# Branch A's scores as two runs of 320 keys in two banks, its filler stages by halves in one bank

## The chip, the cores and the metric

The kernel runs on one core of a Trainium2 chip. The metric is the device time of one launch in microseconds (us), median of the runs. TensorE (PE, with its weight loads shown as PEld) multiplies, VectorE (DVE), ScalarE (ACT) and GpSimd (POOL) work beside it, SyncE (SP) issues weight transfers. Each engine works through its own queue in order, and engines meet by semaphores only.

## The reference

One step of a two-layer backbone (DEPTH 2, width 1024) on 128 context tokens and 512 latent tokens, 640 in all, which is five tiles of 128 (tile 0 context, tiles 1 to 4 latent). Every layer has one input projection that feeds three branches. Branch A, which the change is about, is:

```
def dense_gqa(q, k, v, n_kv, sink=None):          # 8 query heads, 2 key/value heads, head_dim 64
    s = einsum('bqkgd,blkd->bkgql', qblk, k)      # 128 queries at a time
    p = softmax(s)
    return einsum('bkgql,blkd->bqkgd', p, v)
# latent:  a_out = dense_gqa(qa, concat([ka, ka_ctx]), concat([va, va_ctx]), 2)   512 + 128 cached keys
# context: a_out = dense_gqa(qa, ka, va, 2)                                       128 keys
# merge:   g_a, g_b, g_c = split(sigmoid(h @ w_gate + b_gate)); y = (g_a*ya + g_b*yb + g_c*yc) @ w_out
```

Branch B is windowed attention with cached keys and a sink, branch C a gated mixing of chunks. Matrix products are done to nearly full float32 precision by splitting operands into a rounded high part and a low remainder, both fp32r, and multiplying high by high, high by low and low by high.

## The kernel before

All engines walk one written order, `ORDER`, of events such as `("S", l, br, g, i)`; every engine does its own part of each event, in that order. So the place of an event in the order is its place in every queue. A plan (`bank_plan`) gives each stage that TensorE fills one or two of the 8 PSUM banks; TensorE waits (`begin`) until the stage that held the bank before has been read (`wait_drained`).

Branch A works on ten groups of four heads: `GROUPS` are (key/value head, query tile) pairs, tiles 1, 2, 3, 4 for groups 0 to 7 and tile 0 for groups 8 and 9. A latent group has 5 key tiles (4 latent, 1 cached), a context group 1. `attention` makes one step for each key tile of each group, 42 steps in all. Before step 0 stands the entry, with the first scores. Step n holds, in this order:

- `T`: four transposes of the probabilities (PE), which ACT then copies rounded to `p_hi`; DVE makes the remainder (`pl`)
- `S`: at most one score unit of a later group in most steps (PE); DVE takes the maxima and writes `neg`
- `iv`: the inverse of the sum of the unit scored one step before (DVE), and POOL's product of the probabilities with it
- the `O`, `og`, `oh`, `ol` events that finish an output, where due
- `PV`: the two products with the values of step n-2 (PE, `L1110` and `L1111`)
- the filler: work of another stage that keeps TensorE busy
- `ex`: the exponentials of the unit scored in this step (ACT)

The filler of branch A is the gate product of the merge, `z`: seven stages `("z", l, 0, j)`, j from 1 to 7, each 48 matmuls of 320 columns (both halves of the 640 tokens) in 8 chunks of 6 matmuls. A stage takes two banks (6 and 7) and ACT copies both halves out with one instruction (L1365) at the `z` event behind the last chunk. 8 chunks lie in the entry, 43 in the 42 steps, 5 ahead of the last PV.

A latent group has five score units: "cache", the cached keys against all four heads (8 matmuls of 128 columns, L1089 and L1091, two for each head), and one unit for each head (2 matmuls of 512 columns). Each unit takes one bank of two in turn (0 and 1). For a cache unit DVE takes four maxima at once (L1648) and ACT copies the scores to the SBUF tile `cached` (L1300). For a head unit DVE takes the maximum over 512 (L1666) and combines both into `neg` (L1668), and ACT makes two exponentials, of the cached part from `cached` (L1309) and of the 512 from the bank (L1314), each followed by a read of its sum (ACTIVATION_READ_ACCUMULATOR). The bank is free after the second. A group g from 2 to 7 is scored in steps 5g-7 (cache) and 5g-6, 5g-5, 5g-4, 5g-3 (its heads), the last three steps and more ahead of its first T. In the entry stand the cache unit and four heads of group 0 and the cache unit and first head of group 1, and the order there is: filler chunk, `S`, then `ex` and `iv` of the unit before. The other three heads of group 1 come in steps 0 to 2. The first `S` waits until the keys of all latent tiles and of the cache are there (`k_lo`, L1620).

Weight units of the filler go through a ring: ACT rounds `w_hi` (L1154), POOL makes `w_lo` (L1812); these are `split` events, two counted events behind the stage that frees the place, not between the last `S` and `iv` of a group.

The probabilities of a group may be transposed (T) only when POOL has multiplied those of its last head.

## Time and profile before

| | us |
|---|---|
| median of 3 runs (1400.83 to 1403.29) | 1401.62 |
| the profiled execution | 1401.75 |
| its span | 1399.9 |
| branch A, layer 0, first score to the first matmul behind it | 119.5 to 233.0 |
| branch A, layer 1, first score | 808.7 |
| granted TensorE clock, mean | 0.997 |

A timeline row is: start, duration, engine, line, operation, output and inputs, shapes, count; in brackets the idle time before and what ended it. A matmul's duration runs to its modelled end and overlaps the next one, so the time that a matmul takes on TensorE is the distance to the next start. The same holds for ACT and DVE instructions, which overlap by up to some tenths of a microsecond.

### The profile page before, as it was taken

To read this page: it belongs to the slowest core of one execution; us is meant where nothing else is said; L and a number is where in the kernel's file an instruction comes from. 1 tells how busy PE (TensorE), PEld (TensorE's weight loads), DVE (VectorE), ACT (ScalarE), POOL (GpSimd) and SP (SyncE) were. 2 spreads that over 40 slices of the span, in tenths; PEclk is the share of its full clock that TensorE was granted. 3 is DMA by queue.
4 is the path that set the end of the run, shared out by engine and by line. 5 is a ranking of instruction groups with operands and counts; after the bars stand their busy time and mean duration, and the time that the engine had idled before them with its cause. 6 is when DMAs were issued, how large, how long until landed. Compare 5 with 4: busy or idle time off the path is not lost.

```text
span 1399.9 us, 22466 instructions
## 1 busy us (share of the span) xinstructions
PE 1358.6 (97%) x8654; PEld 1256.5 (90%) x8654; DVE 769.3 (55%) x1610; ACT 626.5 (45%) x1304; POOL 682.9 (49%) x490
## 2 busy tenths in 40 slices
PE   7999999999999999999999999999999999999997
PEld 5898989899888899999888988998989989999986
DVE  5656773163874511656685577722458725037558
ACT  4436876234765221223264478852367733122131
POOL 3456565334565354345653566642256554444450
PEclk9999999999999999999999999999999999999999
DMA  9312001122012344354421210012111041225321
GB/s 377 123 61 80 16 31 47 61 80 76 31 47 83 113 154 155 111 198 136 136 100 48 84 61 31 31 46 79 61 61 46 31 136 60 76 76 196 121 90 76
DMA packets 36761, 126.87 MB, mean 91 GB/s; under 512 B 5040, under 2 KB 5808, under 8 KB 36656
## 3 DMA queue, kind: packets, MB, share of 16 engines
q1 hardware_dynamic: 29952, 108.54, 22.8%
q10 hardware_dynamic: 6704, 16.90, 3.3%
q8 instruction: 69, 1.13, 0.3%
q14 instruction: 36, 0.29, 0.1%
HBM read 119.66 MB, written 5.77 MB: 90 GB/s over the span
## 4 chain that ended last, share of the span: by engine, by line
PE 88%; DVE 4%; POOL 2%; ACT 2%; issue 1%; DVEq 0%; ACTq 0%; POOLq 0%
PE ps L952 50%; PE ps L900 7%; PE ps L902 7%; PE ps L901 7%; PE ps L1099 4%; PE ps L1089 3%; PE ps L1091 2%; PE ps L1110 2%; PE ps L1111 2%; PE ps L969 1%; POOL w_lo L1812 1%; POOL p_f_a L1838 1%; PE ps L1118 1%; PE ps L977 1%; PE ps L985 0%
## 5 line engine op out<-in xcount | busy, mean ns | idle before, releaser
L1812 POOL TENSOR_TENSOR w_lo<-raw,w_hi 128x1024 fp32r<-128x1024 f32 x148 | 360.0, 2438 | 267.5 <-ACT w_hi L1154 181.8
L952 PE MATMUL ps<-h_hi,w_hi 128*128 128x320 f32 x1280 | 295.4, 312 | 8.7 <-DVE g_c L1706 4.6
L952 PE MATMUL ps<-h_hi,w_lo 128*128 128x320 f32 x1280 | 291.6, 309 | 0.0
L952 PE MATMUL ps<-h_lo,w_hi 128*128 128x320 f32 x1280 | 291.2, 309 | 0.0
L952 PEld LDWEIGHTS ps<-h_hi,w_hi 128*128 128x128 f32 x1280 | 217.6, 188 | 25.3 <-DVE g_c L1706 6.0
L1154 ACT ACTIVATE w_hi<-raw 128x1024 fp32r<-128x1024 f32 x148 | 154.2, 1055 | 143.1 <-DMA raw<-in_weights 64.3
L952 PEld LDWEIGHTS ps<-h_lo,w_hi 128*128 128x128 f32 x1280 | 214.9, 188 | 1.6
L952 PEld LDWEIGHTS ps<-h_hi,w_lo 128*128 128x128 f32 x1280 | 214.7, 188 | 1.8
L900 PE MATMUL ps<-w_hi,h_hi 128*128 128x512 f32 (+1 forms) x360 | 129.8, 360 | 1.2 <-POOL w_lo L1812 1.0
L902 PE MATMUL ps<-w_hi,h_lo 128*128 128x512 f32 (+1 forms) x360 | 128.3, 356 | 0.0
L901 PE MATMUL ps<-w_lo,h_hi 128*128 128x512 f32 (+1 forms) x360 | 128.1, 356 | 0.0
L1858 POOL TENSOR_TENSOR merge<-merge,gy 128x640 f32<-128x640 f32 x32 | 53.2, 1663 | 140.6 <-DVE gy L1721 140.6
L1838 POOL TENSOR_TENSOR p_f_a<-p_f_a,inv 128x640 f32<-128x640 f32 (+1 forms) x68 | 84.2, 1241 | 66.9 <-DVE inv L1679 66.6
L1721 DVE TENSOR_TENSOR gy<-ps,sg 128x640 f32<-128x640 f32 x32 | 26.3, 821 | 151.6 <-PE ps L952 151.6
L1666 DVE TENSOR_REDUCE top<-ps 128x1 f32<-128x512 f32 (+1 forms) x128 | 84.1, 657 | 30.6 <-PE ps L1091 28.3
L1838 POOL TENSOR_TENSOR p_f_b<-p_f_b,inv 128x512 f32<-128x512 f32 (+1 forms) x68 | 67.0, 1002 | 68.3 <-DVE inv L1679 67.6
L1325 ACT ACTIVATE p_hi<-ps 128x512 fp32r<-128x512 f32 x144 | 85.5, 594 | 26.8 <-PE ps L1099 23.5
L1373 ACT ACTIVATE sg<-ps,pack 128x640 f32<-128x640 f32 x32 | 25.4, 794 | 160.2 <-PE ps L952 160.2
L952 PE MATMUL ps<-o_hi,w_hi 128*128 128x320 f32 x384 | 89.2, 313 | 1.9 <-DVE merge L1714 1.9
L952 PE MATMUL ps<-o_hi,w_lo 128*128 128x320 f32 x384 | 87.5, 309 | 0.0
L952 PE MATMUL ps<-o_lo,w_hi 128*128 128x320 f32 x384 | 87.4, 309 | 0.0
L1089 PE MATMUL ps<-k_hi,q_t 128*128 128x128 f32 (+2 forms) x224 | 80.8, 378 | 5.5 <-ACT p_f_b L1314 2.8
(188 smaller groups left out, 2620.4 us busy)
## 6 DMA issues: line engine op xcount, KB each, us to landing
raw<-in_weights SPq DMA_DIRECT2D x190, 512.0 KB, 3.3
raw_more<-in_weights SPq DMA_DIRECT2D x10, 512.0 KB, 10.2
x<-in_x_sample ACTq DMA_DIRECT2D x6, 512.0 KB, 9.3
x_mid<-x ACTq DMA_DIRECT2D x5, 512.0 KB, 2.6
x<-x_mid ACTq DMA_DIRECT2D x5, 512.0 KB, 7.5
y_sample<-x SPq DMA_DIRECT2D x3, 512.0 KB, 2.6
pack<-in_pack ACTq DMA_DIRECT2D x2, 528.0 KB, 6.3
x<-in_x_sample SPq DMA_DIRECT2D x2, 512.0 KB, 4.8
```

Of the source, the lines that this page charges most:

```text
L900: pe.matmul(out, st_hi, mv_hi, start=start, stop=False)
L901: pe.matmul(out, st_hi, mv_lo, start=False, stop=False)
L902: return pe.matmul(out, st_lo, mv_hi, start=False, stop=stop)
L952: last = pe.matmul(ps[:, s + half, 0:HALF], w[:, u % RING, cols], acts[:, k, half * HALF:(half + 1) * HALF], start=k == 0 and part == 0, s ...
L1089: pe.matmul(ps[:, s, col:col + width], q_t[:, head, t * P:(t + 1) * P], k_hi[:, kv, src], start=True, stop=False)
L1099: last = pe.transpose(ps[:, s, h * P:(h + 1) * P], p_part(br, g)[:, h, i * P:(i + 1) * P], ident)
L1154: did(act.activation(w_hi[:, n % RING, :], raw_tile(r), ACT.Copy), hi_made)
L1325: did(act.activation(p_hi[:, n % 3, :], ps[:, s, :], ACT.Copy), p_hi_made)
L1666: after(did(dve.tensor_reduce(best[:, h:h + 1], ps[:, s, 0:n * P], axis=AX.X, op=ALU.max)))
L1812: did(pool.tensor_tensor(w_lo[:, n % RING, :], raw_tile(r), w_hi[:, n % RING, :], ALU.subtract), w_ready)
L1838: did(pool.tensor_tensor(part, part, inv[:, c, heads].unsqueeze(2).to_broadcast(list(part.shape)), ALU.mult), over_sum)
L1858: did(pool.tensor_tensor(merge[:, j, :], merge[:, j, :], gy[:, j % 2, :], ALU.add), merged)
```

## The change

`in_two_banks`: in a latent group of branch A there is no cache unit. The 512 latent and the 128 cached keys, which lie side by side, are one run of 640 for each head, cut into two runs of 320; each run takes a bank of its own, out of three (0, 1, 2) in turn. DVE takes a maximum of each run and ACT an exponential of each run; the tile `cached`, its copy, and the exponentials from it are gone. Scores are in steps 5g-6 to 5g-3 as before, and step 5g-7 has none. T goes to banks 3 and 4, the output sums to 5 and 6.

`by_halves`: the filler stages have one bank (7) and do first one half of the tokens (4 chunks of 6 matmuls), then the other; ACT copies the first half out at a new event `z1` behind chunk 4, the second at `z` behind chunk 8. Chunk 5 waits for the first copy.

The entry has 11 chunks instead of 8 (40 in the steps, 5 at the end), and in branch A its order is: `S`, two filler chunks (three after the last), `ex`, `iv` of the same unit; nothing stands ahead of the first `S`. It holds the four heads of group 0 and the first of group 1.

```diff
@@ -72,15 +72,28 @@
         return ["heads"]
-    return ["cache", 0, 1, 2, 3] if br == "a" else [0, 1, 2, 3]
+    return [0, 1, 2, 3]
+def in_two_banks(br, g):
+    return br == "a" and GROUPS[g][1] != 0
 def key_run(br, tile):
     if br == "a":
-        return 1, 4, None
+        return 1, 5, None
     return {1: (FRONT, 3, (2, 1, 1)), 2: (FRONT, 4, (1, 0, 3)), 3: (2, 4, (2, 0, 3)), 4: (3, 3, (3, 0, 1))}[tile]
+HALF_CHUNKS = 4
+def by_halves(stage):
+    return stage[0] == "z" and stage[2] == 0 and stage[3] > 0
 def chunks(stage, n):
@@ -108,14 +121,11 @@
         end = max(first[g] - ahead, start)
-        ahead_of_heads = len(units) > GRP and holder >= 0
         for i, e in enumerate(units):
-            n = i - ahead_of_heads
-            at = start - 1 if n < 0 else start + (end - start + 1) * n // (len(units) - ahead_of_heads)
+            at = start + (end - start + 1) * i // len(units)
             scores[at].append(e)
             exps[at].append(("ex", *e[1:]))
-            if score_units(br, g)[e[4]] != "cache":
-                inverses[at if at < 0 else at + 1].append(("iv", *e[1:]))
+            inverses[at if at < 0 else at + 1].append(("iv", *e[1:]))
     filler = list(filler)
@@ -126,14 +136,20 @@
         used[1] = upto
-    for i, e in enumerate(scores[-1]):
+    for i, e in enumerate(scores[-1] if br == "a" else []):
+        out.append(e)
+        out.extend(first_filler[2 * i:2 * i + 2 if i + 1 < len(scores[-1]) else None])
+        out.append(exps[-1][i])
+        out.extend(v for v in inverses[-1] if v[1:] == e[1:])
+    for i, e in enumerate(scores[-1] if br == "b" else []):
         out.extend(first_filler[len(first_filler) * i // len(scores[-1]):len(first_filler) * (i + 1) // len(scores[-1])])
             out.extend(v for v in inverses[-1] if v[1:] == scores[-1][i - 1][1:])
-    out.append(exps[-1][-1])
-    out.extend(v for v in inverses[-1] if v[1:] == scores[-1][-1][1:])
+    if br == "b":
+        out.append(exps[-1][-1])
+        out.extend(v for v in inverses[-1] if v[1:] == scores[-1][-1][1:])
     def product(n):
@@ -279,12 +295,13 @@
                     *whole(("z", l, 0, 0)), queries[4], queries[0]])
-    out.append(("pool", 6, 7))
+    out.append(("pool", 7))
     filler = []
     for j in range(1, KT_D):
-        filler.extend(chunks(("z", l, 0, j), 8))
+        filler.extend(chunks(("z", l, 0, j), HALF_CHUNKS * 2))
+        filler[-1 - HALF_CHUNKS] = (filler[-1 - HALF_CHUNKS], ("z1", l, 0, j))
         filler[-1] = (filler[-1], ("z", l, 0, j))
-    steps = list(flat(attention(l, "a", filler[:8], filler[8:-5], filler[-5:], 2, 3)))
+    steps = list(flat(attention(l, "a", filler[:11], filler[11:-5], filler[-5:], 2, 3)))
     if l == 0:
@@ -530,6 +547,11 @@
             take(("out", e[1], 1, e[2]), 1, until=("out", e[1], 1, e[2]))
+        elif kind == "cr" and by_halves(e[2]):
+            if e[3] == 0:
+                take((*e[2], "first"), 1, 7, until=("z1", *e[2][1:]))
+            elif e[3] == HALF_CHUNKS:
+                take(e[2], 1, 7, until=e[2])
         elif kind == "cr" and e[3] == 0:
@@ -537,14 +559,16 @@
         elif kind == "S":
-            take(e, 1, turn["S"] % 2)
-            turn["S"] += 1
+            stages = [(*e, "first"), e] if in_two_banks(*e[2:4]) else [e]
+            for stage in stages:
+                take(stage, 1, turn["S"] % (3 if e[2] == "a" else 2))
+                turn["S"] += 1
         elif kind == "T":
-            take(e, 1, 2 + turn["T"] % 2)
+            take(e, 1, (3 if e[2] == "a" else 2) + turn["T"] % 2)
             turn["T"] += 1
             stage = ("O",) + e[1:4]
-            take(stage, 1, 4 + turn["O"] % 2, until=stage)
+            take(stage, 1, (5 if e[2] == "a" else 4) + turn["O"] % 2, until=stage)
             turn["O"] += 1
@@ -953,6 +976,24 @@
                     if i == n - 1:
+                        did(last, filled[s])
+                def half_rows(stage, i):
+                    half, u = i // HALF_CHUNKS, USERS[stage]
+                    mine = stage if half else (*stage, "first")
+                    s = PLACE[mine][0]
+                    if i == 0:
+                        pe.wait_ge(w_ready, u + 1)
+                    if i % HALF_CHUNKS == 0:
+                        begin(mine)
+                    work = [(k, part) for k in range(KT_D) for part in range(3)]
+                    each = len(work) // HALF_CHUNKS
+                    for k, part in work[i % HALF_CHUNKS * each:(i % HALF_CHUNKS + 1) * each]:
+                        w, acts = ((w_hi, h_hi), (w_hi, h_lo), (w_lo, h_hi))[part]
+                        last = pe.matmul(ps[:, s, 0:HALF], w[:, u % RING, k * P:(k + 1) * P],
+                                         acts[:, k, half * HALF:(half + 1) * HALF],
+                                         start=k == 0 and part == 0, stop=k == KT_D - 1 and part == 2)
+                    if i % HALF_CHUNKS == HALF_CHUNKS - 1:
                         did(last, filled[s])
@@ -1068,7 +1112,7 @@
                         unit, (kv, t) = score_units(br, g)[i], GROUPS[g]
-                        s = begin(e)
+                        s = begin((*e, "first") if in_two_banks(br, g) else e)
                         if g == 0 and i == 0:
@@ -1078,13 +1122,18 @@
                             wait_drained(pe, ("qt", l, br, t))
-                        if unit in ("heads", "cache"):
-                            place = KEY_PLACE[0 if unit == "heads" else CACHE]
-                            runs = [(kv * GRP + h, h * P, P, place * P) for h in range(GRP)]
+                        if unit == "heads":
+                            runs = [(kv * GRP + h, h * P, P, KEY_PLACE[0] * P) for h in range(GRP)]
+                        elif in_two_banks(br, g):
+                            first = key_run(br, t)[0] * P
+                            runs = [(kv * GRP + unit, 0, HALF, first + half * HALF) for half in range(2)]
                         else:
                             runs = [(kv * GRP + unit, 0, n * P, place * P)]
-                        for head, col, width, key in runs:
+                        for n, (head, col, width, key) in enumerate(runs):
+                            if n and in_two_banks(br, g):
+                                did(last, filled[s])
+                                s = begin(e)
                             src = slice(key, key + width)
@@ -1291,24 +1340,24 @@
                         scores, unit, c = ("S",) + e[1:], score_units(br, g)[i], GROUP_NO[e[1:4]]
-                        s = wait_filled(act, scores)
+                        if not in_two_banks(br, g):
+                            s = wait_filled(act, scores)
                         if l and (br, g, i) == ("a", 0, 0):
                         act.wait_ge(neg_made, NEG_NO[scores])
-                        if unit == "cache":
-                            did(act.activation(cached[:, g % 2, :], ps[:, s, :], ACT.Copy), drained[s])
+                        if in_two_banks(br, g):
+                            for half, stage in enumerate(((*scores, "first"), scores)):
+                                s = wait_filled(act, stage)
+                                did(act.activation(p_part(br, g)[:, unit, half * HALF:(half + 1) * HALF], ps[:, s, 0:HALF], ACT.Exp,
+                                                   bias=neg[:, c % 3, unit:unit + 1],
+                                                   accum_out=sums[:, c % 3, half, unit:unit + 1]), drained[s])
                             continue
                                 act.activation(sums[:, c % 3, 1, h:h + 1], sink[:, head:head + 1], ACT.Exp, bias=bias)
-                            if br == "a" and unit != "heads":
-                                wait_drained(act, ("S", l, br, g, 0))
-                                act.activation(p[:, LAT * P:], cached[:, g % 2, h * P:(h + 1) * P], ACT.Exp, bias=bias,
-                                               accum_out=sums[:, c % 3, 1, h:h + 1])
-                                p = p[:, 0:LAT * P]
                             n = p.shape[-1]
@@ -1358,6 +1407,11 @@
                             drained[s])
+                    elif kind in ("z", "z1") and by_halves(("z", *e[1:])):
+                        _, l, r, j = e
+                        half = int(kind == "z")
+                        s = wait_filled(act, e if half else ("z", l, r, j, "first"))
+                        did(act.activation(merge[:, j, half * HALF:(half + 1) * HALF], ps[:, s, 0:HALF], ACT.Copy), drained[s])
                     elif kind == "z":
@@ -1641,12 +1695,16 @@
                         unit, (kv, t) = score_units(br, g)[i], GROUPS[g]
-                        s = wait_filled(dve, e)
+                        s = None if in_two_banks(br, g) else wait_filled(dve, e)
                         best, others = top[:, c, 0, :], top[:, c, 1, :]
                         sinks = sink[:, kv * GRP:(kv + 1) * GRP]
-                        if unit == "cache":
-                            did(dve.tensor_reduce(others, by_head(ps[:, s, :]), axis=AX.X, op=ALU.max), neg_made)
-                            dve.wait_ge(neg_made, NEG_NO[e])
+                        if in_two_banks(br, g):
+                            for half, stage in enumerate(((*e, "first"), e)):
+                                s = wait_filled(dve, stage)
+                                tok = did(dve.tensor_reduce(top[:, c, half, unit:unit + 1], ps[:, s, 0:HALF], axis=AX.X, op=ALU.max))
+                            after(tok)
+                            did(dve.tensor_scalar(neg[:, c, unit:unit + 1], best[:, unit:unit + 1], others[:, unit:unit + 1], -1.0,
+                                                  ALU.max, ALU.mult), neg_made)
                         elif unit == "heads":
...
```

## Rows read from the trace of the kernel before

**Rows 1.** Part 1 of the page, each engine over the whole span.

```profile
PE 1358.6 (97%) x8654; PEld 1256.5 (90%) x8654; DVE 769.3 (55%) x1610; ACT 626.5 (45%) x1304; POOL 682.9 (49%) x490
```

**Rows 2.** Part 4 of the page, the chain that ended last, by engine.

```profile
PE 88%; DVE 4%; POOL 2%; ACT 2%; issue 1%; DVEq 0%; ACTq 0%; POOLq 0%
```

**Rows 3.** Windows inside branch A: length, busy time (instructions) of each engine, clock, DMA.

```profile
110.00:230.00 120.00, 116.20 (x757) 106.93 (x756) 85.98 (x223) 90.25 (x245) 75.87 (x62) 1.00 0.12 39
820.00:920.00 100.00, 98.80 (x644) 90.83 (x643) 72.04 (x182) 79.05 (x214) 62.34 (x52) 1.00 0.09 30
```

**Rows 4.** Timeline of TensorE, layer 0: chunk, head step, step with cache unit.

```profile
169.54 0.46 PE L952 MATMUL ps<-h_hi,w_hi 128*128 128x320 f32 x2
...
170.42 0.60 PE L1099 MATMUL ps<-ident_r,p_f_a 128*128 128x128 f32 x4
170.78 0.48 PE L1089 MATMUL ps<-k_hi,q_t 128*128 128x512 f32 x1
171.10 0.40 PE L1091 MATMUL ps<-k_lo,q_t 96*128 96x512 f32 x1
171.33 0.40 PE L1110 MATMUL ps<-p_hi,vv 128*128 128x512 f32 x1
...
173.03 0.31 PE L1089 MATMUL ps<-k_hi,q_t 128*128 128x128 f32 x1
...
173.96 0.45 PE L1110 MATMUL ps<-p_hi,vv 128*128 128x512 f32 x1
```

**Rows 5.** Groups by form: count, busy us, mean ns of one, idle before.

```profile
L952 PE MATMUL ps<-h_lo,w_hi 128*128 128x320 f32 x1280 | 291.2, 309 | 0.0
...
L1666 DVE TENSOR_REDUCE top<-ps 128x1 f32<-128x512 f32 x96 | 66.2, 690 | 29.5 <-PE ps L1091 28.3
...
L1314 ACT ACTIVATE p_f_a<-ps,neg 128x512 f32<-128x512 f32 x64 | 43.2, 675 | 0.1
...
L1314 ACT ACTIVATE p_f_b<-ps,neg 128x384 f32<-128x384 f32 x32 | 18.0, 562 | 0.0
L1666 DVE TENSOR_REDUCE top<-ps 128x1 f32<-128x384 f32 x32 | 17.8, 557 | 1.1
...
L1365 ACT ACTIVATE merge<-ps 128x640 f32<-128x640 f32 x16 | 11.3, 704 | 20.8 <-PE ps L952 20.5
```

**Rows 6.** Timeline of ACT and DVE around the end of a filler stage, layer 0.

```profile
168.36 0.70 ACT L1365 ACTIVATE merge<-ps 128x640 f32<-128x640 f32 x1 [0.62 <-PE ps L952]
...
168.96 0.39 ACT L1309 ACTIVATE p_f_a<-cached,neg 128x128 f32<-128x128 f32 x1
...
169.27 0.69 DVE L1666 TENSOR_REDUCE top<-ps 128x1 f32<-128x512 f32 x1 [0.40 <-PE ps L1091]
...
169.91 0.20 ACT L1314 ACTIVATION_READ_ACCUMULATOR p_f_a<-ps,neg 128x1 f32 x1
169.99 0.21 DVE L1668 TENSOR_SCALAR neg<-top 128x1 f32<-128x1 f32 x1
```

**Rows 7.** Timeline of branch B, layer 0: a score that waits for its bank.

```profile
346.08 0.19 ACT L1314 ACTIVATION_READ_ACCUMULATOR p_f_b<-ps,neg 128x1 f32 x1
...
346.32 0.45 PE L1089 MATMUL ps<-k_hi,q_t 128*128 128x384 f32 x1 [0.97 <-ACT p_f_b L1314]
```

**Rows 8.** Timeline of the entry, layers 0 and 1: first score, first maxima, first T.

```profile
119.53 0.30 PE L1089 MATMUL ps<-k_hi,q_t 128*128 128x128 f32 x1 [1.39 <-DVE k_lo L1620]
...
131.13 0.63 PE L1099 MATMUL ps<-ident_r,p_f_a 128*128 128x128 f32 x4 [0.38 <-POOL p_f_a L1838]
...
811.02 0.69 DVE L1648 TENSOR_REDUCE top<-ps 128x4 f32<-128x512 f32 x1
...
820.76 0.63 PE L1099 MATMUL ps<-ident_r,p_f_a 128*128 128x128 f32 x4 [0.38 <-POOL p_f_a L1838]
```

**Rows 9.** Waits of TensorE, whole span: us in total, times, longest.

```profile
PE ps L1099 <- POOL p_f_a L1838: 2.4, 4, 0.8
```

More of the change, by code:

```diff
@@ L738, in build @@
         p_lo_first = {"a": at("p_lo_a", G0, [P, 2, BW], F32R), "b": at("p_lo_b", X0 + 16384, [P, 2, BW], F32R)}
-        cached = at("cached", G0 + 4096, [P, 2, BW])
         o_sum = at("o_sum", A0 + 50176, [P, 2, 2 * P])
@@ L1044, in _ @@
                                 pe.wait_ge(o_done, O_PER_LAYER * l + (10, 20)[stage[2]])
-                        channel_rows(stage, i, n)
+                        if by_halves(stage):
+                            half_rows(stage, i)
+                        else:
+                            channel_rows(stage, i, n)
                     elif kind == "kt":
@@ L1658, in _ @@
                         else:
-                            h, n = unit, len(group_slots(br, g)) - (br == "a")
+                            h, n = unit, len(group_slots(br, g))
                             place, _, mask = key_run(br, t)
@@ L1666, in _ @@
                             after(did(dve.tensor_reduce(best[:, h:h + 1], ps[:, s, 0:n * P], axis=AX.X, op=ALU.max)))
-                            other = others[:, h:h + 1] if br == "a" else sinks[:, h:h + 1]
-                            did(dve.tensor_scalar(neg[:, c, h:h + 1], best[:, h:h + 1], other, -1.0, ALU.max, ALU.mult), neg_made)
+                            did(dve.tensor_scalar(neg[:, c, h:h + 1], best[:, h:h + 1], sinks[:, h:h + 1], -1.0, ALU.max, ALU.mult),
+                                neg_made)
                     elif kind == "iv":
```

## The prediction

> **What bounds the kernel now.** I read the page first. TensorE has matmuls in flight for 97% of the span, no other engine is busy for more than 55% [rows 1], and the chain that ended last runs through TensorE for 88% [rows 2]. Then the windows in branch A: TensorE is busy 116.2 of 120 us and 98.8 of 100 us there, at full clock and with DMA at a tenth [rows 3]. So in this stage a microsecond of TensorE work is a microsecond of time, and so is a microsecond that TensorE waits. But ACT is busy 75 to 79% and DVE 72% [rows 3], above their shares of the whole span. Under TensorE runs a chain score, maximum (DVE), exponential (ACT), product (POOL), and what I must find is how much room it has once a score unit needs the bank of the unit just before it.
>
> **What TensorE's own work costs.** All from starts [rows 4]. A filler chunk of six 320-wide matmuls takes 170.42 - 169.54 = 0.88, so 0.147 each. The transposes T take 0.36. A head unit takes 171.33 - 170.78 = 0.55: 0.32 for the first matmul and 0.23 for the second; the first one behind the transposes pays 0.09 more. The cache unit takes 173.96 - 173.03 = 0.93, eight matmuls at 0.116. A PV pair is 0.47.
>
> After the change a head unit is four 320-wide matmuls: (0.147 + 0.09) + 3 x 0.147 = 0.67, in the entry 0.59. That is 0.12 more than before for each of 64 heads: +7.7. Sixteen cache units go: -14.9. In the step that loses its cache unit PV follows the transposes and pays their 0.09, but no longer the 0.05 it paid behind the 128-wide ones (0.28 against 0.23 for its first matmul), so 12 x 0.04 = +0.5. Together TensorE has 6.7 us less to do. The columns are the same (640 for a head in both); what goes is that a 128-wide matmul costs 0.116 where a quarter of a 512-wide one costs 0.058.
>
> [...]
>
> **How long a score holds its first bank.** Count from the unit's first matmul. The first run is two matmuls; the second starts at 0.24 and its result is there 0.31 later [rows 5]: 0.54, and DVE starts 0.04 after that. A maximum over 384 takes 0.56 and over 512 0.69 [rows 5], so over 320 about 0.49; two of them, overlapping a little, with the wait for the second, 0.95 (bounds: 0.9 without any wait, 1.1 with none of the overlap). Then `neg` 0.21 [rows 6] and 0.09 until ACT starts. The exponentials over 384 and 512 take 0.56 and 0.675 [rows 5], so 320 about 0.51, and the sum's read begins 0.1 before its end and takes 0.19: 0.60. From the end of such a read to the matmul that waited for the bank pass 0.05 (346.27 to 346.32 [rows 7]). Sum: 0.54 + 0.04 + 0.95 + 0.21 + 0.09 + 0.60 + 0.05 = 2.48.
>
> With three banks the second run of the next head needs this bank. TensorE reaches it after 0.67 + 0.47 (PV) + 0.88 (chunk) + 0.36 (T) + 0.38 (first run) = 2.76. So a plain step fits, with 0.28 to spare, where before a head had two steps. That such a wait is real is seen in branch B, with two banks: 0.97 us for one score [rows 7].
>
> **Step by step, the waits this adds.**
>
> Filler halves. `z` or `z1` stands ahead of `ex` in ACT's queue, so ACT sits until the chunk is done. Today that is 168.36, and the exponential behind it starts 0.60 later, at 168.96 [rows 6]; nobody minded, since the bank was needed two units later. Now: chunk done at 0.67 + 0.47 + 0.88 = 2.02, result 0.16 and wait 0.05 later, the copy of 320 holds ACT for 0.35 (it was 0.60 for 640; bounds 0.30 and 0.60), exponential 0.60, 0.05: 3.23 against 2.76, a wait of 0.47, plus 0.1 for a matmul that starts after a wait (0.45 against 0.34 us for a 384-wide one). 0.57 each. Where: with 11 chunks in the entry, chunk 11 + n ends step n (n up to 20), 10 + n from step 22 on, and every fourth ends a half: steps 1, 5, 9, 13, 17, 22, 26, 30, 34, 38. Heads are scored in that step and the next at 1, 5, 9, 26 and 30. So 5 x 0.57 = 2.85 in each layer. The ring's `split` (about 1 us of ACT) falls behind the T copy and ahead of the next `neg`, in time that ACT has free: nothing, unless ACT is late, and then up to 1 us.
>
> Step 0 has neither PV nor a chunk (40 chunks on 42 steps, the first falls in step 1). TensorE is at the second run of the next head after 0.67 + 0.36 + 0.38 = 1.41 instead of 2.76: it waits 2.48 - 1.41 = 1.07 in each layer. Before, that step had a chunk.
>
> The last five chunks stand together, and the first of them ends a half: its copy (0.16 + 0.05 + 0.43 + 0.05, and 0.1) holds TensorE 0.75 in each layer.
>
> The entry. `iv` of a unit stands ahead of the next maximum on DVE and waits for both exponentials. From one unit's first maximum to the next's: 0.95 + 0.21 + 0.09 + 0.52 + 0.60 + 0.05 + 0.33 (sum and inverse) = 2.75, while TensorE offers a unit every 0.59 + 2 x 0.88 = 2.35. On top come `z1` and `z` ahead of the exponentials of the second and fourth head. Followed through, the second runs of units 3, 4 and 5 wait 0.97, 0.38 and 0.96, with restarts 2.5 on 12.6 of work (5 x 0.59 + 11 x 0.88): 15.1 from first score to first T. Before it was 131.13 - 119.53 = 11.6 [rows 8], and three chunks (2.64) that now lie here lay in the steps: 14.24 on the same footing. Layer 0: +0.9. That holds the chunk that ran ahead of the first score and covered part of its wait for `k_lo` [rows 8]; now this wait is bare. In layer 1 DVE is not free for the first maximum before 811.02 [rows 8], whatever TensorE does, so the second run of unit 2 waits until 811.02 + 0.95 + 0.21 + 0.09 + 0.60 + 0.05 = 812.92, and following on from there the first T comes at 825.4 against 820.76 + 2.64 = 823.4: +2.0. Both contain the entry's share of the work saved.
>
> **The sum.** Steps 0 to 41, each layer: work -6 x 0.93 + 27 x 0.12 + 6 x 0.04 = -2.1; waits 1.07 + 2.85 + 0.75 = +4.67; so +2.55, twice 5.1. Entries 0.9 + 2.0. Of the 2.4 us that T waits for POOL [rows 9] about a third goes, because TensorE comes later: -0.8. In all +7.2 on the profiled execution's own 1401.75 (span 1399.9 and 1.85 around it), which lies 0.13 above the median: 1408.8 as a median.
>
> DVE does 0.26 more for each head (0.95 against 0.69) and 0.69 less for each group, in steps of about 2.4 of which it fills 2.0; ACT loses the copy of `cached`. Neither alone becomes the bound; it is the round trip.
>
> **Rivals.** A change within 0.2% (2.8 us) can't be told from none.
>
> A, on the other side: the filler halves cost nothing. ACT would have to be through with the half's copy before `neg` is late, that is the first exponential drained within 2.76 even there. For it: my chain is put together from instructions that overlap, and TensorE has 0.28 to spare. Against it: ACT's wait for the chunk is in today's trace and lies at the end of the step [rows 6]. It decides where the wait at a half falls under about 0.1. Then what stays is the shorter work -6.7, POOL -0.8, step 0 2.1, and about 1 in each entry: 1398. Chance 0.19.
>
> B: the waits are real but half of mine (halves 0.25 each, entries +0.5 each), and meet the gain: 1402. Speaks for it that a late TensorE lets ACT and DVE catch up, and some waits are counted where an earlier one has made room. Chance 0.21.
>
> C, my forecast: work 6.7 less, waits about 14 more: 1408.8, from 1404.5 to 1411. Chance 0.45.
>
> D: the round trip is longer than 2.76 in every step, for instance because the second maximum waits for the second run and ACT is late by T's copy. Each of the 14 further pairs in a layer then waits: at 3.0 that is 28 x 0.2 = 5.6 more, 1414. Against it: the room of 0.28, and 169.27 to 169.99 for a whole maximum [rows 6]. Chance 0.12.
>
> E: TensorE's work does not shrink at all, only the waits come: 1408.8 + 6.7 = 1415.5. [...] Chance 0.03.
>
> **Numbers.** Predicted 1408.8. Slower by over 0.2%: C, D and E, 0.60. Within: B, 0.21. Faster: A, 0.19. The range takes in half of A and half of D: 1396 to 1414. C alone: 1404.5 to 1411.
>
> **What would show it.** The 128-wide score groups gone but for context heads, 320-wide ones at 0.147 apart; TensorE in branch A waiting for ACT's exponentials at the second run, some ten times by half a microsecond behind a half's copy, once by about 1 us in step 1, and in the entry; first T some 15 us behind the first score in layer 0. Wrong if these waits are missing or short (A, B), or stand in nearly every head step (D).

## The result and the profile after

The changed kernel takes 1417.3 us (median of 4 runs, 1415.48 to 1418.5) against 1401.74 on the same chip: ratio 1.0108, interval 1.0096 to 1.012. It is slower, as predicted, but by 15.6 us where 7.2 were predicted, and it lies above the whole stated range (1396 to 1414). The profiled execution took 1417.76, with a span of 1415.7, 15.8 more than before.

The page after, its first part and the shares of the chain that ended last (see [rows 1, 2]):

```profile
PE 1361.5 (96%) x8654; PEld 1261.3 (89%) x8654; DVE 771.7 (55%) x1658; ACT 617.3 (44%) x1302; POOL 683.2 (48%) x490
...
PE 85%; DVE 5%; ACT 3%; POOL 3%; issue 2%; DVEq 0%; ACTq 0%; POOLq 0%
```

TensorE's part of the chain falls from 88 to 85 hundredths, and DVE, ACT, POOL and issue each have one more: TensorE now waits for others more often. Groups by form, with count, busy us, mean ns of one and idle before (see [rows 5]):

```profile
L1352 ACT ACTIVATE p_f_a<-ps,neg 128x320 f32<-128x320 f32 x128 | 66.4, 526 | 26.4 <-DVE neg L1706 25.9
...
L1704 DVE TENSOR_REDUCE top<-ps 128x1 f32<-128x320 f32 x128 | 58.1, 485 | 26.6 <-PE ps L1140 26.4
...
L1414 ACT ACTIVATE merge<-ps 128x320 f32<-128x320 f32 x28 | 12.3, 438 | 39.6 <-PE ps L993 39.4
```

The prices worked out for 320 columns hold: 485 ns for a maximum (0.49 us expected) and 526 for an exponential (0.51). The waits of TensorE over the whole span (us in total, times, longest) say where the time is (see [rows 9]):

```profile
PE ps L1138 <- ACT p_f_a L1352: 9.9, 17, 2.3
...
PE ps L1138 <- DVE k_lo L1674: 2.2, 1, 2.2
...
PE ps L1148 <- DVE p_lo_last L1742: 1.9, 2, 1.0
...
PE ps L1148 <- POOL p_f_a L1896: 1.4, 4, 0.3
...
PE ps L993 <- ACT merge L1414: 1.1, 2, 0.5
```

Score matmuls wait 17 times for an exponential to free their bank. One kind of wait is new and was not foreseen: T (the transposes of the probabilities) for `p_lo_last`, 0.96 us in each layer.

The span in parts, each taken between starts of TensorE's instructions in both traces (branch A ends at the first matmul of L923, L900 before):

| | before | after | predicted difference | measured |
|-|-|-|-|-|
| start to first score, layer 0 | 119.53 | 118.55 | 0 | -1.0 |
| first score to first T, layer 0 | 11.60 | 17.49 | +3.5 | +5.9 |
| first T to the end of branch A, layer 0 | 101.87 | 103.30 | -0.5 | +1.4 |
| from there to the first score, layer 1 | 575.68 | 574.55 | -0.9 | -1.1 |
| first score to first T, layer 1 | 12.08 | 19.90 | +5.5 | +7.8 |
| first T to the end of branch A, layer 1 | 101.9 | 103.27 | -0.5 | +1.4 |
| the rest | 477.24 | 478.64 | 0 | +1.4 |

(Predicted differences are the prediction's terms on this footing: three chunks, 2.64 us, count in the entry, and its 0.8 of relief from POOL is split over the layers.) The entries miss by 2.4 and 2.3, the steps by 1.9 twice, the rest by 1.4, and the first scores give 1.2 back: 8.7 of the 8.6 us that are missing.

Of what the first scores give back, 1.0 in layer 0 is chance and not the change. In the profiled execution of the kernel before, TensorE ran at a granted clock of 0.50 for 3.4 us from 26.3 on, and in that of the changed kernel it did not. Of the twelve profiled executions of this document, the six without that stretch have their first score at 118.3 to 118.6, whatever the kernel; five of the six with it at 119.5 to 119.7 (the sixth has more dummies in front of it).

**In the entries TensorE's clock falls.** Windows of the entries: length, busy time (instructions) of PE, PEld, DVE, ACT and POOL, granted clock (1.00 is full speed), DMA share, GB/s. First the changed kernel, where TensorE stood 2.24 us ahead of 118.55 and 2.35 us ahead of 819.12:

```profile
118.00:120.00 2.00, 1.46 (x5) 1.49 (x6) 0.69 (x3) 0.08 (x1) 2.00 (x1) 0.50 0.63 176
120.00:122.00 2.00, 2.00 (x9) 2.00 (x9) 0.77 (x3) 1.13 (x4) 2.00 (x2) 0.50 0.68 207
122.00:124.00 2.00, 2.00 (x9) 2.00 (x8) 0.58 (x3) 0.00 (x0) 1.66 (x2) 0.50 0.69 207
124.00:126.00 2.00, 2.00 (x15) 2.00 (x14) 0.92 (x3) 0.00 (x0) 0.00 (x0) 0.98 0.51 197
...
825.00:827.00 2.00, 2.00 (x9) 2.00 (x9) 0.53 (x3) 1.13 (x4) 0.61 (x2) 0.50 0.00 0
```

The same stretch of the kernel before:

```profile
120.00:122.00 2.00, 2.00 (x16) 1.91 (x15) 0.69 (x1) 0.56 (x1) 2.00 (x2) 1.00 0.62 223
```

PE is busy for all of 2.00 us in both. Only the count tells them apart, 9 matmuls against 16, and the clock column, 0.50 against 1.00. A busy share alone would have hidden this. Timeline of the changed kernel, TensorE, layer 0: start, duration, and in brackets the idle time before and what ended it (see [rows 8]).

```profile
118.55 0.61 PE L1138 MATMUL ps<-k_hi,q_t 128*128 128x320 f32 x1 [2.24 <-DVE k_lo L1674]
...
119.75 0.47 PE L993 MATMUL ps<-h_hi,w_hi 128*128 128x320 f32 x1
120.02 0.47 PE L993 MATMUL ps<-h_lo,w_hi 128*128 128x320 f32 x1
...
124.20 0.31 PE L993 MATMUL ps<-h_lo,w_hi 128*128 128x320 f32 x1
124.35 0.31 PE L993 MATMUL ps<-h_hi,w_lo 128*128 128x320 f32 x1
...
136.04 0.60 PE L1148 MATMUL ps<-ident_r,p_f_a 128*128 128x128 f32 x4
136.40 0.39 PE L1138 MATMUL ps<-k_hi,q_t 128*128 128x320 f32 x1
...
137.08 0.60 PE L1148 MATMUL ps<-ident_r,p_f_a 128*128 128x128 f32 x4
137.44 0.39 PE L1138 MATMUL ps<-k_hi,q_t 128*128 128x320 f32 x1
...
138.82 0.41 PE L1138 MATMUL ps<-k_hi,q_t 128*128 128x320 f32 x1 [0.84 <-ACT p_f_a L1352]
...
140.10 0.60 PE L1148 MATMUL ps<-ident_r,p_f_a 128*128 128x128 f32 x4
```

A 320-wide matmul takes 0.27 at the half clock (119.75 to 120.02) and 0.15 at the full one (124.20 to 124.35). The head unit is 137.08 - 136.40 = 0.68, as predicted (0.67). Step 0 has no chunk, and the head scored in step 1 has its second run at 138.82 where it could start at 137.44 + 0.38 = 137.82. The first matmul after this wait takes 0.25 to the next start (138.82 to 139.07) where 0.15 is usual, 0.1 more (the restart), so that step is 1.1 longer (predicted 1.07).

**A half's copy ahead of an exponential.** Timeline of the changed kernel, all engines, at the end of a filler half (see [rows 6]):

```profile
148.16 0.89 DVE L1704 TENSOR_REDUCE top<-ps 128x1 f32<-128x320 f32 x2 [0.64 <-PE ps L1140]
149.08 0.21 DVE L1706 TENSOR_SCALAR neg<-top 128x1 f32<-128x1 f32 x1
149.80 0.44 ACT L1414 ACTIVATE merge<-ps 128x320 f32<-128x320 f32 x1 [1.24 <-PE ps L993]
150.14 0.52 ACT L1352 ACTIVATE p_f_a<-ps,neg 128x320 f32<-128x320 f32 x1
150.55 0.20 ACT L1352 ACTIVATION_READ_ACCUMULATOR p_f_a<-ps,neg 128x1 f32 x1
150.80 0.41 PE L1138 MATMUL ps<-k_hi,q_t 128*128 128x320 f32 x1 [0.31 <-ACT p_f_a L1352]
```

`neg` is there at 149.29, but ACT stands 1.24 us for the end of the chunk, copies the half, and starts the exponential at 150.14. From T to T these steps take 2.96, 2.95, 2.78, 2.95 and 2.96, where a plain head step takes 2.38: 2.69 in the layer, predicted 2.85.

**Where a copy delays the context heads.** The same kernel, steps 34 to 37:

```profile
219.74 0.44 ACT L1414 ACTIVATE merge<-ps 128x320 f32<-128x320 f32 x1 [2.55 <-PE ps L993]
220.08 0.36 ACT L1363 ACTIVATE p_f_a<-ps,neg 128x128 f32<-128x128 f32 x1
...
222.82 0.64 ACT L1374 ACTIVATE p_hi<-ps 128x512 fp32r<-128x512 f32 x1
...
223.50 0.69 DVE L1742 TENSOR_TENSOR p_lo_last<-ps,p_hi 128x512 fp32r<-128x512 f32 x1 [3.86 <-ACT p_hi L1374]
224.24 0.66 PE L1148 MATMUL ps<-ident_r,p_f_a 128*128 128x128 f32 x4 [0.96 <-DVE p_lo_last L1742]
```

Here the copy stands ahead of the exponentials of the context heads (tile 0, one bank for four heads). They come late, so the rounding copy `p_hi` behind them does, so does DVE's remainder, and T of step 37 waits for it: 2.91 from T to T against 1.78, 1.13 in each layer. Two experiments below bear this out: with the copy behind these exponentials, or with the half's end moved to another step, this T is on time (in the first of these a chunk waits 0.9 for the copy instead).

### The profile page after: what moved, and what is told of

Its sections match the earlier page's. It is cut to its first block, busy times and chain, and to the rows that moved or that the text cites. A ratio compares the mean times of both kernels' runs of the same rounds, so it can differ in the third digit from the quotient of the medians.

```text
span 1415.7 us, 22482 instructions
## 1 busy us (share of the span) xinstructions
PE 1361.5 (96%) x8654; PEld 1261.3 (89%) x8654; DVE 771.7 (55%) x1658; ACT 617.3 (44%) x1302; POOL 683.2 (48%) x490
## 3 DMA queue, kind: packets, MB, share of 16 engines
q8 instruction: 69, 1.13, 0.3%
## 4 chain that ended last, share of the span: by engine, by line
PE 85%; DVE 5%; ACT 3%; POOL 3%; issue 2%; DVEq 0%; ACTq 0%; POOLq 0%
PE ps L975 44%; PE ps L923 7%; PE ps L925 7%; PE ps L924 7%; PE ps L993 6%; PE ps L1148 4%; PE ps L1138 3%; PE ps L1140 2%; PE ps L1159 2%; PE ps L1160 2%; PE ps L1010 1%; POOL p_f_a L1896 1%; POOL w_lo L1870 1%; POOL with_eps L1854 1%; PE ps L1167 1%
## 5 line engine op out<-in xcount | busy, mean ns | idle before, releaser
L975 PE MATMUL ps<-h_hi,w_hi 128*128 128x320 f32 x1056 | 243.6, 312 | 8.4 <-DVE g_c L1764 4.3
L975 PE MATMUL ps<-h_lo,w_hi 128*128 128x320 f32 x1056 | 240.7, 309 | 0.0
L975 PE MATMUL ps<-h_hi,w_lo 128*128 128x320 f32 x1056 | 240.5, 309 | 0.0
L975 PEld LDWEIGHTS ps<-h_hi,w_hi 128*128 128x128 f32 x1056 | 176.6, 188 | 15.9 <-DVE g_c L1764 5.7
L975 PEld LDWEIGHTS ps<-h_hi,w_lo 128*128 128x128 f32 x1056 | 177.3, 188 | 1.8
L975 PEld LDWEIGHTS ps<-h_lo,w_hi 128*128 128x128 f32 x1056 | 177.4, 188 | 1.6
L923 PE MATMUL ps<-w_hi,h_hi 128*128 128x512 f32 (+1 forms) x360 | 129.2, 359 | 1.2 <-POOL w_lo L1870 1.0
L1138 PE MATMUL ps<-k_hi,q_t 128*128 128x320 f32 (+3 forms) x224 | 82.3, 376 | 15.9 <-ACT p_f_a L1352 9.9
L1352 ACT ACTIVATE p_f_a<-ps,neg 128x320 f32<-128x320 f32 x128 | 66.4, 526 | 26.4 <-DVE neg L1706 25.9
```

The lines of the kernel that those rows point to most:

```text
L923: pe.matmul(out, st_hi, mv_hi, start=start, stop=False)
L975: last = pe.matmul(ps[:, s + half, 0:HALF], w[:, u % RING, cols], acts[:, k, half * HALF:(half + 1) * HALF], start=k == 0 and part == 0, s ...
L1138: pe.matmul(ps[:, s, col:col + width], q_t[:, head, t * P:(t + 1) * P], k_hi[:, kv, src], start=True, stop=False)
L1352: did(act.activation(p_part(br, g)[:, unit, half * HALF:(half + 1) * HALF], ps[:, s, 0:HALF], ACT.Exp, bias=neg[:, c % 3, unit:unit + 1], ...
```

## The experiments

The theory at this point: the waits of the round trip in the steps are one part, and entries lengthened by waits and by the clock that falls with them the other. The rivals: the entry's order alone, the smaller banks of the halves, or TensorE's work not having shrunk.

**The copy of a half moved behind the exponentials.**

```diff
+def copy_behind_exps(steps):
...
+        if held and e[0] != "ex":
+            out.extend(held)
+            held = []
+        if e[0] in ("z", "z1"):
+            held.append(e)
...
-    steps = list(flat(attention(l, "a", filler[:11], filler[11:-5], filler[-5:], 2, 3)))
+    steps = copy_behind_exps(flat(attention(l, "a", filler[:11], filler[11:-5], filler[-5:], 2, 3)))
```

> The changed kernel with one thing moved: ACT's copies of the filler halves (z1, z) stand behind the exponentials of their step instead of ahead of them. Theory (a score's second run waits because ACT sits at the half's copy before it frees the first bank): the five waits of 0.57 in each layer go, so do about 0.7 for each of the two halves that end in the entry, and the 1.0 us wait for p_lo_last in the steps of the context scores: about 4.5 us a layer, 1408 in all. Rival (the loss is the entry's order and the lower clock there alone): no change, 1417.

Measured 1409.01 (before 1401.52), ratio 1.0054 (1.0039 to 1.0069); predicted 1408. From the first T to the end of branch A 101.4 in both layers, 1.9 less than after. Waits of TensorE in it:

```profile
PE ps L1006 <- ACT merge L1427: 5.5, 11, 0.9
...
PE ps L1151 <- ACT p_f_a L1365: 4.8, 5, 2.3
```

Seventeen waits for the exponential (9.9 us) became five (4.8), and those for `p_lo_last` (1.9) and for POOL in the steps (1.4) went. But the waits for the copy rose from two (1.1) to eleven (5.5) and took over half of it back: chunks of the next half found their bank not copied. The entry of layer 0 took 15.06 with 3.4 us at half clock, that of layer 1 16.82 at full clock, together 5.5 less than after, of the 9.8 by which its span (1405.9) is shorter. Part of these 5.5 is the clock, which fell for 6.8 us in both entries of the changed kernel, and not the copy's place.

**The entry in the order of before, the rest as changed.**

```diff
-    for i, e in enumerate(scores[-1] if br == "a" else []):
-        out.append(e)
-        out.extend(first_filler[2 * i:2 * i + 2 if i + 1 < len(scores[-1]) else None])
-        out.append(exps[-1][i])
-        out.extend(v for v in inverses[-1] if v[1:] == e[1:])
-    for i, e in enumerate(scores[-1] if br == "b" else []):
+    for i, e in enumerate(scores[-1]):
```

> The changed kernel with the entry's order of before (filler chunks, score, then exponential and inverse of the unit before), still 11 chunks there. [...] Rival (three banks are too few for any order, the waits move to the next place): under 3 us gained.

Measured 1415.29, ratio 1.0094 (1.0078 to 1.0111): 2.0 less than the changed kernel, which is not clear of noise, as the intervals overlap; 1409 was expected, with each entry 3 to 5 us shorter, so this missed. The first score waits less (0.48, two chunks stand ahead of it), but now the products come late:

```profile
135.41 0.84 PE L1142 MATMUL ps<-ident_r,p_f_a 128*128 128x128 f32 x4 [2.67 <-POOL p_f_a L1890]
```

and the clock falls to 0.50 for 3.4 us behind this wait, in both layers. So going back to the old order does not repair the entry: either order has a wait of over 2 us.

**Only the filler by halves, on the kernel before.**

```diff
+HALF_CHUNKS = 4
...
+        filler.extend(chunks(("z", l, 0, j), HALF_CHUNKS * 2))
+        filler[-1 - HALF_CHUNKS] = (filler[-1 - HALF_CHUNKS], ("z1", l, 0, j))
```

> The kernel before (cache unit, two score banks, old entry with 8 chunks) with only the filler stages by halves in one bank. Theory: with two units of room for every score bank the earlier copies hurt nobody; only the wait of the last five chunks for the first half's copy comes, 0.5 to 0.8 a layer, so about 1403. Rival (the halves cost by themselves, through ACT's queue or the single bank): the 2.9 us a layer of the forecast, 1407 or more.

Measured 1404.51 (10 runs; before 1401.52), ratio 1.002 (1.0011 to 1.003); expected 1403. The halves alone cost 3 us: 1.4 in each layer between first T and end, 1.11 of it a wait of the last five chunks for a half's copy (1.4 with the restart). The waits of 0.5 for a score's bank at a half's end are not there: the halves alone do not make them.

**Keeping TensorE busy in front of layer 0's first score.** The kernel has two dummy events there, each of two 128-wide matmuls whose result nobody reads; first 22 events, then 10.

```diff
-        steps.insert(steps.index(("S", l, "a", 0, 0)), ("warm", 2, 5))
+        steps.insert(steps.index(("S", l, "a", 0, 0)), ("warm", 22, 5))
```

> The changed kernel with 22 instead of 2 dummy matmuls of 128 columns ahead of layer 0's first score, where TensorE waits 2.2 us for k_lo. [...] Rival (the entry is bound by DVE and ACT anyway): under 0.7 us.

> The changed kernel with 10 instead of 2 dummy matmuls ahead of layer 0's first score; at 0.224 us each they end about when k_lo is there, so the first score is not later. Theory (the lower clock of layer 0's entry costs 2.4 us): 1415 with the first T of layer 0 some 15.1 us behind the first score instead of 17.5. Rival (the slow stretch hides behind DVE and ACT): 1417.

With 22: 1415.92, ratio 1.0104 (1.0089 to 1.0119); about 1415 was expected, with the clock at 1.00 in layer 0 and its entry 2 to 2.6 us shorter. The dummies took 5.17 us and moved the first score 3.1 later (of which 1.1 is the early stretch at half clock told of above, which this execution has), but behind it the clock stayed at 1.00 and the entry took 15.05. With 10: 1414.18, ratio 1.0092 (1.0077 to 1.0108), 3.1 less than the changed kernel. The intervals of all three overlap, so the case rests on the traces. Timeline with 10 and a window of it:

```profile
118.37 0.39 PE L1138 MATMUL ps<-k_hi,q_t 128*128 128x320 f32 x1 [0.47 <-DVE k_lo L1674]
...
133.41 0.60 PE L1148 MATMUL ps<-ident_r,p_f_a 128*128 128x128 f32 x4
```

```profile
120.00:122.00 2.00, 2.00 (x15) 2.00 (x14) 0.77 (x5) 1.13 (x4) 2.00 (x1) 1.00 0.55 211
```

Same work, same order, first score at nearly the same time (118.37 and 118.55): 15.04 instead of 17.49. All of the difference lies in the first 20 matmuls, which take 3.04 here and 5.47 in the changed kernel. So 2.4 us of the entry of layer 0 are the clock. The prediction had 15.1. In layer 1 nothing was changed, and yet the execution with 22 kept its clock:

```profile
819.38 0.42 PE L1138 MATMUL ps<-k_hi,q_t 128*128 128x320 f32 x1 [2.34 <-ACT p_f_a L1352]
```

The wait is the same 2.34, and the entry took 17.65 at full clock (predicted 17.6); with 3.4 us at half clock (the execution with 10) it took 19.18, and in the changed kernel, with 6.8, 19.90.

**ACT copies a half between the two exponentials of the next head.**

```diff
...
+                        if nxt[0] == "ex" and in_two_banks(*nxt[2:4]):
+                            late.append(e)
+                        else:
+                            copy_half(e)
```

> The changed kernel with ACT's copy of a finished filler half put between the two exponentials of the score unit that follows it in the order (the copies that no such unit follows stay). So the first bank is freed before the copy and the next chunk still finds its bank. Theory (the copy's place ahead of the first exponential is what costs 0.57 at five places a layer): those waits go without the new waits of chunks that the place behind both exponentials brought; the entry loses 1.2 a layer too; 1408 in all, and no more than 1409. Rival (ACT is simply too full): the waits come back elsewhere, 1412 or more.

Measured 1407.42 (before 1401.8), ratio 1.004 (1.0026 to 1.0054); expected 1408. From first T to the end 100.4 in both layers, 2.9 less than after: the five waits are gone (2.38 to 2.52 where 2.78 to 2.96 stood), T's two waits for POOL in the steps are gone with them, and only the chunk in the tail still waits for a copy (0.53, as in the changed kernel). The waits of steps 1 (3.01), 22 (3.03) and 37 (2.91) stay, as they should.

**Two chunks of the entry moved into the steps, so that no head step is empty.**

```diff
-    steps = list(flat(attention(l, "a", filler[:11], filler[11:-5], filler[-5:], 2, 3)))
+    steps = list(flat(attention(l, "a", filler[:9], filler[9:-5], filler[-5:], 2, 3)))
```

> The changed kernel with 9 filler chunks in the entry and 42 in the steps, one in each, instead of 11 and 40. Theory: the waits of 1.1 behind step 0 and 0.6 behind step 21, which have no chunk, go; but the first T comes 1.8 earlier by TensorE's own work and then waits about 0.9 for POOL's product of group 0's last head, so about 1.6 in both layers together, 1415.7. Rival (the room of 0.28 us in a plain step is not enough, so chunks matter everywhere or nowhere): no change.

Measured 1417.86, ratio 1.0116 (1.0102 to 1.0129); expected 1415.7, a miss. The waits of steps 1 and 22 went (2.24 and 2.38 from T to T), but the shorter entry left its products late: T waits for POOL six times, 3.2 us in all. Layer 1's entry kept its clock in this execution behind a wait of 2.34, but 12 us later, at 832, the clock fell to 0.50 for 3.4 us behind a wait of only 0.94. A chunk moved between entry and steps moves the wait with it.

**All together: a chunk ahead of the first score, nine behind, four at the end, the copy in between.**

```diff
+        if not i:
+            out.extend(first_filler[:1])
...
-    steps = list(flat(attention(l, "a", filler[:11], filler[11:-5], filler[-5:], 2, 3)))
+    steps = list(flat(attention(l, "a", filler[:10], filler[10:-4], filler[-4:], 2, 3)))
...
```

> Both halves and both runs kept, the order repaired: copies between the exponentials, one filler chunk ahead of the first score again, 10 chunks in the entry, one in each of the 42 steps, 4 at the end so that a half does not end there. Theory: the 6.7 us less of TensorE work are left, with some 3 us of waits in the entries: 1398. Rival (the three score banks cost in every step): 1402 or more.

Measured 1399.16 (11 runs), ratio 0.9984 (0.9975 to 0.9992), expected 1398: faster than before, by 2.6 us. Entries 13.02 and 14.73, both at a granted clock of 1.00. First T to end is 98.5 against 101.9; two chunks fewer than before lie in this stretch (1.76), and the other 1.6 are work that TensorE no longer has, and waits.

**The kernel "all together" with two chunks ahead of the first score; and in a second kernel also the inverses of the first three heads behind the next score (the last two lines).**

```diff
+        counts = (2, 2, 2, 2, 1, 1)
+        if not i:
+            out.extend(first_filler[:counts[0]])
...
+        if 0 < i < 4:
+            out.extend(v for v in inverses[-1] if v[1:] == scores[-1][i - 1][1:])
```

> e7_all with its 10 entry chunks dealt 2 ahead of the first score, then 2, 2, 2, 1, 1 behind the scores (e7_all: 1, then 2, 2, 2, 2, 1). Theory (in the entry a half that ends inside a pair of chunks makes the next chunk wait 0.5 for its copy, and a later first score waits less for k_lo in layer 0 and for DVE in layer 1): two waits of 0.5 a layer go and about 0.4 to 0.9 of the wait behind the first score; 1397 to 1398, against 1399.2. Rival (the round trip of DVE and ACT sets the entry's length whatever TensorE does between): 1399.

> e9_two_ahead with the inverses of the first three heads put behind the next head's score in the order, as before the change, the exponentials staying ahead of it. Theory (the inverse ahead of the next maximum stretches the round trip to 2.75 us, more than the 2.35 in which TensorE offers a unit): up to 0.4 for each of three heads and layer, 2 us less than e9_two_ahead. Rival (with a chunk ahead and full clock the round trip is hidden, or the product of the last head then comes later and the first T waits): no difference.

The first: 1400.13 (11 runs; before 1401.98), ratio 0.9987 (0.9978 to 0.9996), where 1397 to 1398 was expected. Its wait for `k_lo` is down to 0.46 and the two waits for a half's copy in the entry (0.53 and 0.62 in "all together") are gone, but the round trip took it back, and T waits for POOL besides:

```profile
PE ps L1141 <- ACT p_f_a L1363: 1.5, 2, 1.1
PE ps L1151 <- POOL p_f_a L1910: 0.9, 1, 0.9
PE ps L1141 <- DVE k_lo L1688: 0.5, 1, 0.5
```

So the first is no gain on "all together", a miss. The second keeps `iv`, which waits for both exponentials, out of the way of the next maximum on DVE. The same view (waits of layer 0's entry):

```profile
PE ps L1154 <- POOL p_f_a L1913: 0.9, 1, 0.9
PE ps L1144 <- DVE k_lo L1691: 0.5, 1, 0.5
PE ps L1144 <- ACT p_f_a L1366: 0.2, 1, 0.2
```

1.5 us of waiting for exponentials became 0.2. It takes 1397.38 (6 runs), ratio 0.9969 (0.9957 to 0.998), 2.75 below the one without it and 4.6 below the kernel before: the fastest version of all. Entries 12.08 and 12.71, first T to end 98.3. It is the change's own idea with most of its waits taken out; so in the entry the place of `iv` did cost.

## Why the prediction was wrong, and where it was right

The step that failed first is the price of a bare wait. The prediction put the waits ahead of and behind the first score at their length alone and had no term for the clock behind them; the traces show 4.7 us there. The second is the list of waits in the steps, which left out 0.65 and 1.13 us in each layer.

- **What bounds it**: right. Each wait of TensorE in branch A was time, and waits taken out in the experiments came off the time where no other took their place.
- **TensorE's own work**: right. Head unit 0.68 against 0.67, plain head step 2.38. With nearly all waits gone, the last version runs from first T to end in 98.3; with the two chunks (1.76) that it has fewer there that is 100.1 against 101.9 before, 1.8 less (predicted 2.1 for the steps' work), with some 0.3 more waiting left in it than in the kernel before (an estimate from the usual distance between the same pairs of matmuls in both traces). Rival E is out. The 128-wide score matmuls that are gone took 0.116 us each in the kernel before, against 0.058 for a quarter of a 512-wide one [rows 4], and the 320-wide ones take 0.15 here (136.63 to 136.78).
- **Round trip**: right: 2.42 measured from the first matmul of step 21's head to the one in step 22 that reuses its bank, against 2.48:

```profile
185.61 0.39 PE L1138 MATMUL ps<-k_hi,q_t 128*128 128x320 f32 x1
...
188.03 0.42 PE L1138 MATMUL ps<-k_hi,q_t 128*128 128x320 f32 x1 [0.38 <-ACT p_f_a L1352]
```

  Plain head steps fit in 2.76, so rival D is out.
- **Waits at filler halves**: right, 2.69 in a layer against 2.85. The experiment with the copy between the exponentials removes them. Rivals A and B are out.
- **Step 0**: right, 1.1 against 1.07. **The last five chunks**: a wait of 0.53, with the restart 0.80, against 0.75 (the terms written down for it add up to 0.79).
- **"Step 0 has neither PV nor a chunk"**: this failed to ask for a second one. 40 chunks on 42 steps leave two steps empty; the other is step 21, and its successor takes 3.03 instead of 2.38: 0.65 in each layer, left out of the sum.
- **The list of halves that meet a scored head** took only heads in two banks. The copy of step 34 meets the context heads, and 1.13 in each layer came through ACT, `p_hi`, and DVE to T. The prediction asked who waits for the exponential; it did not ask who stands behind it in ACT's queue.
- **"Of the 2.4 us that T waits for POOL about a third goes"**: the waits fell from 2.4 to 1.4 us, but as time the 0.8 did not come. The first T no longer waits, and the entry's own sum held that already. In the steps one long wait (0.81, 0.97 with its restart) became two of 0.34 (0.50 each): 1.0 in a layer, as before. Both come of the copy ahead of the exponentials; with the copy between or behind them they are gone.
- **The entry**: its working was right (15.1 against 15.04 at full clock; 17.6 against 17.65), the sum was not. The term for the clock is missing: the prediction made "this wait is bare" a price of its length alone. Around waits of 2.24 and 2.35 us TensorE's granted clock fell to 0.50 for 6.8 us each time, and that was 2.4 and 2.3 us, the largest part of the miss. For layer 0 it is shown by the ten dummies. For layer 1 the price rests on executions that had the same wait and kept the clock; that the wait is what lets the clock fall there was not tested. The clock also differs from launch to launch: the four launches of the changed kernel had mean clocks of 0.993, 0.996, 0.996 and 0.992, and the profiled one is of the lower kind. Without the 4.7 it would have come out at about 1413 (an estimate), inside the stated range but still 4 above the forecast.
- **The rest of the span**: 1.4 more, of which 0.9 is a wait of TensorE for `merge` (DVE) in layer 1's stage behind branch A:

```profile
955.16 0.82 DVE L1772 TENSOR_TENSOR merge<-ps,merge 128x640 f32<-128x640 f32 x1 [6.25 <-PE ps L975]
956.04 0.42 PE L975 MATMUL ps<-o_hi,w_hi 128*128 128x320 f32 x1 [0.92 <-DVE merge L1772]
```

  It stands in every kernel with the scores in two runs, the fastest too, and not when only the filler is by halves. The kernels' own bank plans account for it. In every kernel with this wait `bank_plan` gives the product `("y", 1, 0, 1)` banks 6 and 7, which `("y", 1, 0, 0)` has just left and DVE is still reading. In the other two it gives banks that an earlier stage has left. So the change also moved a bank far behind the stage that it edits. No run changed the plan there.

In sum: clock 4.7, steps 3.8, the rest 1.4, less 1.2 from earlier first scores, of which 1.0 is the chance told of above. The 1.9 of the steps in a layer are 0.65 + 1.13 + 0.4 for POOL, less 0.16 at the halves; the 0.1 over is not traced.

## What to carry to other kernels

When units come closer together on the same banks, work out the round trip of a bank and hold it against every gap between reuses, the odd ones too: steps without filler, the entry, the tail; and behind every instruction that is made late, follow its own queue, not only who reads its result. A wait of TensorE like those of 2.2 to 2.7 us here, in a stage that ran dense, cost its length and up to 2.4 us more for the clock around it; a forecast should carry both cases. After a change of banks, look also at which banks later stages now get. The cheapest repair was to move work of an off-path engine (a copy, an inverse) from ahead of the instruction that frees the bank to behind it.

## What the runs showed of the hardware

During or just behind a wait of TensorE of 2.2 to 2.7 us in these entries the granted clock fell to 0.50 in eight of twelve cases, each time for 3.4 or 6.8 us, and did not in four, all of them waits of 2.34 to 2.36 in layer 1. In the kernel before and the four experiments whose longest wait in the entries was 1.5 us it did not fall there at all. The fall behind a wait of 0.94, told of above, is the only one in these entries behind a shorter wait.

At 0.50 a 320-wide matmul takes 0.267 instead of 0.147 from start to start (twelve of them in 3.20 us in the changed kernel, 119.75 to 122.95, and in 1.76 in the one with ten dummies, 119.05 to 120.81). What the clock cost in layer 0 is just that: 1.3 of the 6.8 us lay inside the wait, and the matmuls started in the rest took 2.4 us longer. In layer 1 it was 2.3 for 6.8 us, with a later wait shortened from 0.74 to 0.50, and 1.5 for 3.4 us.
